# Packed weight tiles in layer 1, queries ahead of gates and values in the stick-breaking units, and each head's keys dealt out behind the queries of the head before

## The chip, the cores and the metric

The kernel runs on one core of one Trainium2 chip. The metric is the device time of one execution in microseconds (us), as the median of several. Everything is float32 in and out; a product of two float32 matrices is made of three matmuls of rounded parts (high x high, high x low, low x high), so each operand that enters TensorE is first split into a high and a low part.

## The reference, cut to what matters

Two layers over 16 learned meta tokens and 1024 tokens of width 1024. Layer 0 projects the input once and runs four heads of differential attention (A) and eight heads of stick-breaking attention (B) beside each other. Layer 1 is multi-head latent attention (C) of eight heads. Each has a gated output projection and a residual layer norm.

```python
def even_layer(x, ...):                       # layer 0
    qa, ka, va, ga, qs, ks, vs, gs = split_cols(x @ w_in, EVEN_SPLITS)
    ...
    # A: softmax of two maps, w = p[0] - lam * p[1]; rms_norm; * silu(ga)
    # B: z = q k / 8; skip = log_sigmoid(-z) over earlier keys
    log_pass = lax.cumsum(log_skip, axis=3, reverse=True) - log_skip
    a = jnp.where(earlier, jnp.exp(jax.nn.log_sigmoid(z) + log_pass), 0.0)
    ...
    return jnp.concatenate([ya, ys], axis=-1) @ w_out

def odd_layer(x, ...):                        # layer 1
    cq, ckv, k_pe, g = split_cols(x @ w_in, ODD_SPLITS)
    q = (rms_norm(cq, q_norm) @ w_uq).reshape(bsz, L, 8, 128 + 64)
    q = jnp.concatenate([q[..., :128], rope(q[..., 128:], pos)], axis=-1)
    kv = (rms_norm(ckv, kv_norm) @ w_ukv).reshape(bsz, L, 8, 128 + 128)
    ...
    return o @ w_out                          # after softmax, @ v, * silu(g)
```

## The kernel before

All tokens (1040 columns) stay in SBUF with the feature on the partitions. A projection (`project`, line 1941) is the product of one weight tile of 128 output features, with 8, 4 or 2 tiles of 128 input rows (`KT_OF`), and a chunk of 352, 344 or 344 columns (`CHUNKS`); each input tile costs three matmuls, so a chunk is 24, 12 or 6 matmuls. Projections go to two PSUM banks in turn, in their order in `PROJ` (`TURN_BANK`), and one may start once the step before the last has been evacuated (`bank_free`). ACT writes the high part (`proj_hi`) and DVE the low part (`proj_evac`).

Weight tiles (`WEIGHTS`, in order of use) are loaded by SP's queue into `wraw`, split by POOL (`split_weights`, lines 1032 and 1033) into `wsp`, and both have two slots. A split waits until the tile two places before in that order has been used up.

Layer 0 has eight units: 0 to 3 are the A heads, 4 to 7 are pairs of B heads. A unit has keys `k0`, values `v0`, queries `q0` and a gate `g0` of three chunks each, and the A units have a sum of squares `rms0` for a norm of their output. Of the queries there is one buffer, `qst`: a chunk is evacuated to half of its partitions, and POOL copies it to the others (`copy_queries`, line 1134) before scores (line 2009) may read it. For a B unit POOL also makes differences of neighbouring values (`step_values`) before the values are transposed (line 1980). Blocks of 128 queries are taken in pairs: scores of a block, sigmoid on ACT, a scan along the keys on DVE (line 1723), transposes of the weights on TensorE (line 2029), evacuation of these into `ring`, high part by ACT (line 1424) and low part by DVE (line 1738), and the product with the values (line 2059). The scores of blocks 5 to 7 need the third chunk of queries.

Layer 1 has, for each head u, keys `kn`, values `vn` and plain queries `qn`, and for each pair of heads rotated queries `qr`. A rotated chunk is copied by ACT into `rtmp` (line 1342), rotated there and spread by DVE (lines 1556 to 1609), and copied by POOL; there is one `rtmp`. `qh` is the buffer of the plain queries, written by ACT (line 1346) and DVE (line 1614), and is also single. The softmax weights are divided by their sum on POOL (line 1222).

`before_attention` and `in_attention` write down the order of the projections. `weave` then deals them out between the steps of the attention: it is a planner that plays all five engines with a cost for each step, and the order that comes out, for every engine, is fixed in the program. Projections are its fillers: TensorE takes one matmul of them where no score, transpose or product is ready. For the last two units it also deals out the first output blocks of the layer (`FILLS`: the meta block, called 8, and block 0, 48 matmuls of 512 columns each, line 2085), whose weights are eight tiles loaded and split in the meantime (`out_weight`, lines 1367, 1076 and 1777).

## Time and profile before

| | |
|---|---|
| median of 3 runs | 1376.29 us (1375.99 to 1381.58) |
| the profiled execution | 1376.59 us, its span 1374.8 us |
| layer 0: start, projections and attention | 0 to 660 us |
| layer 0 output blocks, layer 1 input projections, norms | 660 to 940 us |
| layer 1 attention | 940 to 1284 us, with some output work from 1270 us on |
| layer 1 output blocks | to the end |

Starts of rows are counted from the start of the span. A row that merges several instructions of one line gives their number behind x; the idle time in brackets is that of the engine just ahead of the row's first instruction, with what released it. PE is TensorE and PEld its weight loads, DVE is VectorE, ACT is ScalarE and POOL is GpSimd.

### The profile page before, as it was taken

The page shows a single profiled execution, that of the slowest core. Times are in us where ns is not written, and L with a number is a line of the kernel's source. Part 1 is how long each engine was busy: PE and PEld are TensorE (multiplying, and loading weights), DVE is VectorE, ACT ScalarE, POOL GpSimd, SP SyncE. Part 2 cuts the span into 40 slices and gives each one's busy share as a digit, 9 for nine tenths or more (in the row PEclk, how much of TensorE's full clock was granted, in tenths as well). Part 3 has the DMA queues.
Part 4 walks back from the last instruction along what each step waited for, and adds up shares of the span by engine and source line. Part 5 has one row for each costly group of instructions (what it writes and reads, how often), then busy time and mean ns, then how long its engine had stood idle before and what let it go on. Part 6 is the DMA issues. An engine that isn't in the chain of part 4 may idle for free.

```text
span 1374.8 us, 22469 instructions
## 1 busy us (share of the span) xinstructions
PE 1320.7 (96%) x8400; PEld 1243.6 (90%) x8400; DVE 874.2 (64%) x1973; ACT 546.1 (40%) x1290; POOL 487.3 (35%) x465
## 2 busy tenths in 40 slices
PE   8999999999899999997999999998999999999997
PEld 7999999999799999996888999998998999989886
DVE  5675869595587847668466323554767676676455
ACT  3443545463545535355111011533444555546200
POOL 3323232223234232347333323563433233334541
PEclk9999999999999999998999999999999999999999
DMA  6000111001011011113133211222111111205242
GB/s 221 32 32 31 47 32 40 23 31 47 32 39 40 20 43 51 60 40 123 58 123 132 93 46 41 83 81 73 36 47 39 51 41 58 66 22 177 78 163 76
DMA packets 47355, 88.26 MB, mean 64 GB/s; under 512 B 4480, under 2 KB 30080, under 8 KB 47120
## 3 DMA queue, kind: packets, MB, share of 16 engines
q1 hardware_dynamic: 44800, 78.45, 17.2%
q10 hardware_dynamic: 2448, 8.39, 1.6%
q8 instruction: 67, 1.10, 0.3%
q14 instruction: 40, 0.33, 0.1%
HBM read 66.84 MB, written 19.98 MB: 63 GB/s over the span
## 4 chain that ended last, share of the span: by engine, by line
PE 51%; DVE 5%; ACT 2%; issue 2%; POOL 1%; DMA 0%; SPq 0%; DVEq 0%; ACTq 0%; POOLq 0%
PE bank L1941 20%; PE bank L2085 14%; PE bank L2009 7%; PE bank L2059 5%; PE bank L2029 4%; ACT rtmp L1342 1%; PE bank L2107 1%; PE bank L1980 1%; DVE qpe L1605 0%; DVE rtmp L1558 0%; DVE qpe L1609 0%; DVE ring L1738 0%; DVE rtmp L1557 0%; DVE pb L1723 0%; DMA woraw<-in_wo 0%
## 5 line engine op out<-in xcount | busy, mean ns | idle before, releaser
L1941 PE MATMUL bank<-big,wsp 128*128 128x344 f32 (+2 forms) x3024 | 560.4, 328 | 15.2 <-DVE qh L1614 7.2
L1941 PEld LDWEIGHTS bank<-big,wsp 128*128 128x128 f32 x3024 | 481.7, 189 | 22.0 <-DVE qh L1614 10.5
L1032 POOL TENSOR_SCALAR wsp<-wraw 128x1024 fp32r<-128x1024 f32 (+3 forms) x92 | 84.9, 923 | 538.7 <-PE bank L1941 422.3
L1738 DVE TENSOR_TENSOR ring<-bank,ring 128x256 fp32r<-128x256 f32 (+3 forms) x292 | 156.9, 553 | 85.1 <-ACT ring L1424 82.5
L1424 ACT ACTIVATE ring<-bank 128x256 fp32r<-128x256 f32 (+3 forms) x292 | 138.6, 495 | 147.1 <-PE bank L2029 106.7
L2085 PE MATMUL bank<-big,wsp 128*128 128x512 f32 x816 | 195.9, 399 | 0.0
L1033 POOL TENSOR_TENSOR wsp<-wraw,wsp 128x1024 fp32r<-128x1024 f32 (+3 forms) x92 | 184.6, 2007 | 7.7
L2059 PE MATMUL bank<-ring,vtok 128*128 128x256 f32 (+2 forms) x1276 | 183.1, 280 | 4.2 <-DVE ring L1738 2.6
L2085 PEld LDWEIGHTS bank<-big,wsp 128*128 128x128 f32 x816 | 153.5, 190 | 35.1 <-DVE big L1777 0.2
L2059 PEld LDWEIGHTS bank<-ring,vtok 128*128 128x128 f32 (+1 forms) x1276 | 171.8, 191 | 10.0 <-issue 4.0
L1941 PE MATMUL bank<-h1t,wsp 128*128 128x344 f32 (+2 forms) x1080 | 173.9, 322 | 1.4 <-DVE lraw L1595 1.4
L1941 PEld LDWEIGHTS bank<-h1t,wsp 128*128 128x128 f32 x1080 | 170.2, 188 | 3.6 <-DVE lraw L1595 1.7
L2029 PE MATMUL bank<-eye,pb 128*128 128x128 f32 (+1 forms) x892 | 134.5, 274 | 11.3 <-DVE ring L1738 6.3
L2029 PEld LDWEIGHTS bank<-eye,pb 128*128 128x128 f32 (+1 forms) x892 | 103.1, 140 | 19.2 <-DVE ring L1738 8.3
L2009 PE MATMUL bank<-kst,qst 128*128 128x264 f32 (+9 forms) x480 | 104.3, 328 | 9.2 <-POOL qst L1134 8.2
L1723 DVE TENSOR_TENSOR_SCAN pb<-tb,distt 128x144 f32<-128x144 f32 (+4 forms) x72 | 100.6, 1409 | 5.6 <-PE bank L2029 3.7
L1222 POOL TENSOR_SCALAR pb<-pb,stat 128x144 f32<-128x144 f32 (+5 forms) x96 | 57.5, 609 | 109.7 <-DVE stat L1729 68.0
L2009 PEld LDWEIGHTS bank<-kst,qst 128*128 128x128 f32 x480 | 76.1, 189 | 21.2 <-POOL qst L1134 12.4
L1414 ACT ACTIVATE pb<-bank,stat 128x144 f32<-128x144 f32 (+6 forms) x112 | 59.7, 540 | 75.8 <-DVE stat L1694 57.8
L2009 PE MATMUL bank<-kh,qh 128*128 128x144 f32 (+6 forms) x336 | 73.4, 327 | 1.2 <-ACT pb L1414 0.8
L1805 DVE SCALAR_TENSOR_TENSOR res<-xres,bank 128x512 f32<-128x512 f32 (+1 forms) x34 | 21.9, 683 | 78.3 <-PE bank L2085 46.6
L1442 ACT ACTIVATE small<-small,eps 128x1 f32<-128x1 f32 (+1 forms) x17 | 5.0, 295 | 167.0 <-DVE small L1824 167.0
(133 smaller groups left out, 1432.5 us busy)
## 6 DMA issues: line engine op xcount, KB each, us to landing
wraw<-in_w SPq DMA_DIRECT2D x47, 512.0 KB, 3.5
wraw<-y_scratch SPq DMA_DIRECT2D x17, 448.0 KB, 3.6
woraw<-in_wo SPq DMA_DIRECT2D x12, 512.0 KB, 5.5
y_scratch<-ot SPq DMA_DIRECT2D x40, 128.0 KB, 1.7
xres<-in_x SPq DMA_DIRECT2D x8, 512.0 KB, 4.7
h_scratch<-res ACTq DMA_DIRECT2D x8, 512.0 KB, 2.6
gate_scratch<-gtmp SPq DMA_DIRECT2D x8, 512.0 KB, 2.9
gate<-gate_scratch SPq DMA_DIRECT2D x8, 512.0 KB, 3.6
```

Of the source, the lines that this page charges most:

```text
L1032: pool.wait_ge(S["pool_step"], tick(nc.gpsimd.tensor_scalar(hi, raw, 1.0, 1.0, ALU.mult, ALU.mult)))
L1033: return nc.gpsimd.tensor_tensor(lo, raw, lo_hi(hi), ALU.subtract)
L1222: nc.gpsimd.tensor_scalar(p_, p_, stat[:, t % 4, 13:14], 1.0, ALU.mult, ALU.mult)\
L1414: A(weights_of(1, slice(0, 128), g, slot, c0, c0 + w), bank[S_BANK[b]][:, 0:w], ACT.Exp, bias=st_(6, 7), scale=SCALE192, accum_out=st_(8 + ...
L1424: A(R[0:rows, r % NRING, 0, 0:w], bank[T_BANK[t]][0:rows, 0:w], ACT.Copy).then_inc(S["tr_hi"], 1)
L1723: V.tensor_tensor_scan(P[:, 0:n][:, ::-1], skip[:, ::-1], distt[0:rows, k0:k0 + n][:, ::-1], 1.0, ALU.mult, ALU.max).then_inc(S["p_ready_d ...
L1738: V.tensor_tensor(R[0:rows, r % NRING, 1, 0:w], bank[T_BANK[t]][0:rows, 0:w], lo_hi(R[0:rows, r % NRING, 0, 0:w]), ALU.subtract).then_inc( ...
L1941: ins = mm(dst, wsp[:, SLOT[kind, u], a, k, :], rhs[:, b, k0 + k, c0:c0 + w], start=(k == 0 and a == 0 and b == 0), stop=last)
L2009: ins = mm(dst, l, r, start=(k == 0), stop=(k == len(prods) - 1))
L2029: ins = nc.tensor.transpose(bank[T_BANK[t]][0:wide, at:at + rows], weights_of(layer, slice(0, rows), g, slot, k0, k0 + wide), eye[0:rows, ...
L2059: ins = mm(PO[:, o0:o0 + wide], l, B["ring"][0:rows, r % NRING, part, at:at + wide], start=(k == 0 and tile == turns[0][0] and part == 0 a ...
L2085: ins = mm(out_bank(n, half)[:, :], wsp[:, SLOT["y", n], a, k, :], wok[:, c, k, 512 * half:512 * half + 512], start=(k == tiles[0] and a = ...
```

## The change

Three things are changed, and no product is added or left out.

1. Layer 1's weight tiles are packed: keys and values of a head are one tile (`kv`, 4 input tiles), rotated and plain queries are one tile for an even head (`qq`, 8 input tiles), and an odd head's plain queries are a tile of 4. `TILE_STEPS` lists the projections that use a tile, and a slot is free after the last of them. Of 28 loads and splits in the attention of layer 1, 16 are left, of the same size together.
2. In layer 0, unit 4's queries stand around the gate of unit 3 (`q[:1] + g[:1] + q[1:] + g[1:]`), and in the B units each unit's next queries stand ahead of and between its values (`q[:1] + v[:1] + q[1:] + v[1:]`), where they stood behind all of them.
3. In layer 1, one chunk of the next head's keys stands behind each chunk of a head's queries, then come the values of the next head. In head 0 its own values take the place of the keys.

The host packs the weights into three arrays for this: `wukv[u]` (keys and values), `wuq_0` (even heads) and `wuq_1` (odd heads).

```diff
@@ -123,6 +123,19 @@
          "kn": KVL_T, "vn": KVL_T, "qn": QL_T, "qr": QL_T}
 
 
+def tile_of(kind, u):
+
+    return ("kv", u) if kind in ("kn", "vn") else ("qq", u) if kind in ("qn", "qr") else (kind, u)
+
+
+def tile_kt(kind, u):
+    return 2 * KVL_T if kind == "kv" else QL_T * (2 - u % 2) if kind == "qq" else KT_OF.get(kind, KD)
+
+
+def kt_before(kind, u):
+    return KVL_T if kind == "vn" else QL_T * (1 - u % 2) if kind == "qn" else 0
+
+
 def proj(kind, u):
     return [("P", kind, u, c) for c in range(len(CHUNKS))]
 
...
@@ -223,21 +236,35 @@
             k, v, q = (proj(kind, u + 1) if u + 1 < UNITS else [] for kind in ("k0", "v0", "q0"))
             norm = proj("rms0", u - 1) if 1 <= u <= A_UNITS else []
             g = proj("g0", u)
-            out += k + v[:1] + norm[:2] + v[1:2] + norm[2:] + v[2:] + proj("g0", u) + q if u < A_UNITS else k[:1] + norm + g[:1] + k[1:] + g[1:] + v + q
+            if u == A_UNITS - 1:
+                g = q[:1] + g[:1] + q[1:] + g[1:]
+                q = []
+            out += k + v[:1] + norm[:2] + v[1:2] + norm[2:] + v[2:] + g + q if u < A_UNITS else k[:1] + norm + g[:1] + k[1:] + g[1:] + q[:1] + v[:1] + q[1:] + v[1:]
         return out
-    out = queries(0, slice(0, None)) + proj("vn", 0)
-    for u in range(1, HEADS):
-        out += proj("kn", u) + proj("vn", u) + queries(u, slice(0, None))
+    out = []
+    for u in range(HEADS):
+        q, more = queries(u, slice(0, None)), proj("vn", 0) if u == 0 else []
+        more += proj("kn", u + 1) + proj("vn", u + 1) if u + 1 < HEADS else []
+        n = len(q) // len(CHUNKS)
+        for c in range(len(CHUNKS)):
+            out += q[n * c:n * c + n] + more[c:c + 1]
+        out += more[len(CHUNKS) * 1:]
     return out
 
 
 BEFORE, WITHIN = [before_attention(n) for n in range(2)], [in_attention(n) for n in range(2)]
 PROJ = [s for s in BEFORE[0] + WITHIN[0] + BEFORE[1] + WITHIN[1] if s[0] == "P"]
-TILES = [[s[1:3] for s in BEFORE[n] + WITHIN[n] if s[0] == "P" and s[1] != "rms0" and s[3] == 0] for n in range(2)]
+TILE_STEPS = {}
+for _s in PROJ:
+    if _s[1] != "rms0":
+        TILE_STEPS.setdefault(tile_of(*_s[1:3]), []).append(_s)
+TILES = [list(dict.fromkeys(tile_of(*s[1:3]) for s in BEFORE[n] + WITHIN[n] if s[0] == "P" and s[1] != "rms0"))
+         for n in range(2)]
 O_STEPS = [("O", 0, b) for b in [META_Q] + list(range(NB))] + [("O", 1, b) for b in range(NB)]
 O_AT = {s: n for n, s in enumerate(O_STEPS)}
 WEIGHTS = TILES[0] + [("y", n) for n in range(NB + 1)] + TILES[1] + [("y", n) for n in range(NB + 1, 2 * NB + 1)]
 WEIGHT_AT = {s: n for n, s in enumerate(WEIGHTS)}
+WEIGHT_AT |= {s[1:3]: WEIGHT_AT[tile] for tile, steps in TILE_STEPS.items() for s in steps}
 STATIONARY = WEIGHTS
 WO_ORDER = [list(range(KD)), [6, 7, 4, 5, 0, 1, 2, 3]]
 OUT_TILES = [[k for k in order if k < KD - 1] + [KD - 1] for order in WO_ORDER]
...
@@ -450,14 +477,14 @@
 
         kind, u = WEIGHTS[n]
         slot_of = WEIGHTS[n - 2]
-        end = ("P", *slot_of, 2) if slot_of[0] != "y" else O_STEPS[slot_of[1]]
+        end = TILE_STEPS[slot_of][-1] if slot_of[0] != "y" else O_STEPS[slot_of[1]]
         done = [("pe", end)] if end in within or end in FILLS[layer] else []
         stored = []
         if kind == "y":
             stored = [("sp", ("Y", unit_groups(layer, UNITS - 2)[-1]))]
         if n >= first_w + 2:
             L.put("sp", "L", ("LW", n), 65, ([("pool", ("V" if slot_of[0] == "y" else "W", n - 2))] if n - 2 >= first_split else []) + stored, 6500 if kind == "y" and layer else 4500)
-        kt = KT_OF.get(kind, KD)
+        kt = tile_kt(kind, u)
         L.put("pool", "W", ("W", n), 430 * kt, ([("sp", ("LW", n))] if n >= first_w + 2 else []) + done, 70)
         if kind == "y":
             last = ("Y", group_of(layer, O_STEPS[u][2]))
...
@@ -610,7 +637,7 @@
          for n in range(2) for k in range(KD)}
 PTURN = {s: n for n, s in enumerate(PROJ)}
 N_CONSTS = 6
-SLOT = {s: n % 2 for n, s in enumerate(STATIONARY)}
+SLOT = {s: n % 2 for s, n in WEIGHT_AT.items()}
 TURN_BEFORE, TURN_BANK = {}, {}
 _bank_turns = {}
 for _s in PROJ:
...
@@ -877,12 +904,9 @@
                 return w1[QL_T + KVL_T]
             if kind == "g1":
                 return w1[QL_T + KVL_T + 1 + u]
-            if kind == "qn":
-                return wuq_n[u]
-            if kind == "qr":
-                return wuq_r[u // 2]
-            return wukv[u, 0 if kind == "kn" else 1]
-
+            if kind == "qq":
+                return (wuq_1 if u % 2 else wuq_0)[u // 2]
+            return wukv[u]
 
         LAST0 = last_turn("g0", UNITS - 1)
         LAST1 = last_turn("qn", HEADS - 1)
...
@@ -911,7 +935,7 @@
                         dst = wraw[:, n % 2, 0:(KD - 1) * 128].rearrange("p (k c) -> p k c", k=KD - 1)
                         src = yd[layer, 0:KD - 1, :, c0:c0 + 128].rearrange("u p c -> p u c")
                     else:
-                        dst, src = wraw[:, n % 2, 0:KT_OF[kind] * 128], w_src(kind, u)
+                        dst, src = wraw[:, n % 2, 0:tile_kt(kind, u) * 128], w_src(kind, u)
                     sp.dma_start(dst, src).then_inc(slot("w_raw", n), 16)
                     issued[0] += 1
 
...
@@ -1038,14 +1062,14 @@
                     n = split_[0]
                     kind, u = WEIGHTS[n]
                     arrived(pool, "w_raw", n)
-                    kt, i = KT_OF.get(kind, KD - 1), STATIONARY.index((kind, u))
+                    kt, i = KD - 1 if kind == "y" else tile_kt(kind, u), STATIONARY.index((kind, u))
                     if i >= 2:
 
                         before = STATIONARY[i - 2]
                         if before[0] == "y":
                             pool.wait_ge(S["y_done"], before[1] + 1)
                         else:
-                            pool.wait_ge(S["proj_done"], last_turn(*before) + 1)
+                            pool.wait_ge(S["proj_done"], PTURN[TILE_STEPS[before][-1]] + 1)
                     ins = split(wsp[:, i % 2, 0, 0:kt, :], wsp[:, i % 2, 1, 0:kt, :],
                                 wraw[:, n % 2, 0:kt * 128].rearrange("p (k c) -> p k c", k=kt))
                     split_[0] += 1
...
@@ -1938,7 +1962,7 @@
                         pe.wait_ge(S["x_split"], X_FIRST[k, c0] + 1)
                     for a, b in ((0, 0), (0, 1), (1, 0)):
                         last = k == kt - 1 and a == 1
-                        ins = mm(dst, wsp[:, SLOT[kind, u], a, k, :], rhs[:, b, k0 + k, c0:c0 + w],
+                        ins = mm(dst, wsp[:, SLOT[kind, u], a, kt_before(kind, u) + k, :], rhs[:, b, k0 + k, c0:c0 + w],
                                  start=(k == 0 and a == 0 and b == 0), stop=last)
                         if last:
                             ins.then_inc(S["proj_done"], 1)
```

The planner makes a new order of all engines from this, beginning with the first queries of unit 4. From the product `X 86 0`, the first of the last head but for its early steps, TensorE's order is as before. Three places follow, all on TensorE, first as before and then as changed (line numbers of the changed kernel are 24 higher here).

The scores of unit 4 of layer 0: `big,wsp` is a projection, `sq,ones` a sum of squares, `kst,qst 128x392` the first scores that read the third chunk of queries. Before:

```order
L1941 MATMUL bank0<-big,wsp 128x352 x4
L2029 MATMUL bank6<-eye,pb 128x128 x2
L1941 MATMUL bank0<-big,wsp 128x352
L2029 MATMUL bank5<-eye,pb 128x128 x3
L1941 MATMUL bank0<-big,wsp 128x352 x19
L1954 MATMUL bank1<-sq,ones 128x352
L2009 MATMUL bank4<-kst,qst 128x392 x2
L2009 MATMUL bank2<-kst,qst 128x392 x2
L2009 MATMUL bank3<-kst,qst 128x328 x2
```

Changed:

```order
L2033 MATMUL bank3<-kst,qst 128x328 x2
L1965 MATMUL bank0<-big,wsp 128x344 x5
L2053 MATMUL bank6<-eye,pb 128x128 x2
L1965 MATMUL bank0<-big,wsp 128x344 x2
L2053 MATMUL bank5<-eye,pb 128x128 x3
L1965 MATMUL bank0<-big,wsp 128x344 x12
L1965 MATMUL bank1<-big,wsp 128x344
L2033 MATMUL bank4<-kst,qst 128x392 x2
L2033 MATMUL bank2<-kst,qst 128x392 x2
L2033 MATMUL bank3<-kst,qst 128x328 x2
```

Before, a chunk of keys of the next unit (128x352) and a sum of squares stand ahead of these scores; the third chunk of queries ends just ahead of the keys. Now a chunk of unit 3's gate (24 matmuls of bank 0, the last 19 of them here) and the first matmul of another stand there, and the queries ended ahead of that chunk.

The end of layer 0's attention, unit 7: `128x512` is the output block 8, `eye,pb` transposes of weights, `ring,vtok` products. Before:

```order
L2059 MATMUL bank7<-ring,vtok 128x256 x7
L2059 MATMUL bank7<-ring,vtok 128x128
L2059 MATMUL bank7<-ring,vtok 128x256
L2059 MATMUL bank7<-ring,vtok 128x128
L2029 MATMUL bank5<-eye,pb 128x128 x4
L2029 MATMUL bank6<-eye,pb 128x128 x3
L2029 MATMUL bank5<-eye,pb 128x128 x2
L2059 MATMUL bank7<-ring,vtok 128x256 x10
L2085 MATMUL bank0<-big,wsp 128x512 x3
L2085 MATMUL bank1<-big,wsp 128x512 x3
```

Changed:

```order
L2053 MATMUL bank6<-eye,pb 128x128 x2
L2109 MATMUL bank0<-big,wsp 128x512
L2053 MATMUL bank5<-eye,pb 128x128 x4
L2033 MATMUL bank4<-kst,qst 128x344 x2
L2033 MATMUL bank2<-kst,qst 128x344 x2
L2109 MATMUL bank0<-big,wsp 128x512 x2
L2109 MATMUL bank1<-big,wsp 128x512 x3
L2109 MATMUL bank0<-big,wsp 128x512
L2033 MATMUL bank3<-kst,qst 128x456 x2
L2033 MATMUL bank4<-kst,qst 128x456 x2
```

Before, the first output matmuls stand behind the last scores, among the transposes of the last pairs but one; now they begin ahead of the scores of 344 and 456 columns, and go on between all that follows.

The start of layer 1's attention, head 0: rotated (336 or 344 columns, 12 matmuls), plain (12) and, changed, values (6). Before:

```order
L1941 MATMUL bank0<-big,wsp 128x336 x12
L1941 MATMUL bank1<-big,wsp 128x336 x12
L1941 MATMUL bank0<-big,wsp 128x344 x12
L1941 MATMUL bank1<-big,wsp 128x344 x4
L2009 MATMUL bank2<-kh,qh 128x144 x3
L2009 MATMUL bank2<-kpe,qpe 128x144
L2009 MATMUL bank2<-kpe2,qpe 128x144
L2009 MATMUL bank3<-kh,qh 128x272 x3
L2009 MATMUL bank3<-kpe,qpe 128x272
L2009 MATMUL bank3<-kpe2,qpe 128x272
L1941 MATMUL bank1<-big,wsp 128x344 x8
L1941 MATMUL bank0<-big,wsp 128x344 x12
```

Changed:

```order
L1965 MATMUL bank0<-big,wsp 128x336 x12
L1965 MATMUL bank1<-big,wsp 128x336 x12
L1965 MATMUL bank0<-big,wsp 128x352 x6
L1965 MATMUL bank1<-big,wsp 128x344 x4
L2033 MATMUL bank2<-kh,qh 128x144 x3
L2033 MATMUL bank2<-kpe,qpe 128x144
L2033 MATMUL bank2<-kpe2,qpe 128x144
L2033 MATMUL bank3<-kh,qh 128x272 x3
L2033 MATMUL bank3<-kpe,qpe 128x272
L2033 MATMUL bank3<-kpe2,qpe 128x272
L1965 MATMUL bank1<-big,wsp 128x344 x8
L1965 MATMUL bank0<-big,wsp 128x344 x12
```

The rotated second chunk took bank 0, in which the rotated first chunk had been. It now takes bank 1, in which the plain first chunk was, and six matmuls of values (128x352) stand between.

## Rows read from the trace of the kernel before

**Rows 1.** The page: busy time, share of the span, instructions.

```profile
PE 1320.7 (96%) x8400; PEld 1243.6 (90%) x8400; DVE 874.2 (64%) x1973; ACT 546.1 (40%) x1290; POOL 487.3 (35%) x465
```

**Rows 2.** TensorE's waits, 300 to 660 us: total us, times, longest.

```profile
PE bank L2009 <- POOL qst L1134: 7.5, 6, 2.7
PE bank L2029 <- DVE ring L1738: 6.3, 5, 3.1
PE bank L1954 <- ACT sq L1354: 1.2, 1, 1.2
```

**Rows 3.** TensorE's waits, 938 to 1232 us.

```profile
PE bank L1941 <- DVE qh L1614: 7.2, 8, 1.7
...
PE bank L1941 <- DVE rtmp L1556: 1.3, 2, 0.6
PE bank L1941 <- POOL wsp L1033: 1.2, 1, 1.2
PE bank L2009 <- ACT pb L1414: 0.8, 1, 0.8
PE bank L1941 <- DVE kh L1612: 0.2, 1, 0.2
```

**Rows 4.** Timeline of TensorE: start, us, operation, count, idle before; first and last of four.

```profile
360.10 1.27 PE L2009 MATMUL bank<-kst,qst 128*128 128x392 f32 x6 [2.66 <-POOL qst L1134]
...
608.31 1.29 PE L2009 MATMUL bank<-kst,qst 128*128 128x392 f32 x6 [1.21 <-POOL qst L1134]
```

**Rows 5.** Windows: length, busy PE, PEld, DVE, ACT, POOL, clock, DMA, GB/s.

```profile
626.20:640.00 13.80, 10.14 (x57) 8.22 (x57) 10.67 (x16) 12.67 (x21) 13.44 (x8) 0.88 0.54 186
640.00:650.00 10.00, 6.37 (x38) 5.82 (x37) 9.94 (x10) 3.59 (x8) 10.00 (x3) 0.78 0.34 101
650.00:660.50 10.50, 10.50 (x64) 9.25 (x64) 6.75 (x10) 3.00 (x6) 5.12 (x3) 0.89 0.19 61
```

**Rows 6.** Timeline of TensorE, runs of one kind.

```profile
319.95 1.52 PE L2059 MATMUL bank<-ring,vtok 128*128 128x256 f32 x12
321.31 0.83 PE L2029 MATMUL bank<-eye,pb 128*128 128x128 f32 x6
...
576.67 13.38 PE L1941 MATMUL bank<-big,wsp 128*128 128x344 f32 x83
...
660.55 14.83 PE L2085 MATMUL bank<-big,wsp 128*128 128x512 f32 x63
```

**Rows 7.** Timeline of POOL in unit 4, and stepped values in unit 5.

```profile
353.77 3.22 POOL L1033 TENSOR_TENSOR wsp<-wraw,wsp 128x1024 fp32r<-128x1024 f32 x1
357.13 2.92 POOL L1134 TENSOR_SCALAR qst<-qst 64x688 fp32r<-64x688 f32 x2
...
415.32 1.92 POOL L1162 TENSOR_TENSOR sq<-vt 128x1039 f32<-128x1039 f32 x1
```

**Rows 8.** DVE's groups of 626.2 to 660.5 us, then timelines of DVE and POOL.

```profile
L1738 DVE TENSOR_TENSOR ring<-bank,ring 128x512 fp32r<-128x512 f32 (+2 forms) x18 | 10.1, 590 | 4.7 <-ACT ring L1424 4.7
...
634.45 2.31 DVE L1723 TENSOR_TENSOR_SCAN pb<-tb,distt 128x1040 f32<-128x1040 f32 x1
...
641.98 3.64 DVE L1723 TENSOR_TENSOR_SCAN pb<-tb,distt 128x1040 f32<-128x1040 f32 x1
...
636.98 2.36 POOL L1076 TENSOR_TENSOR big<-pre_values,big 128x1024 fp32r<-128x1024 f32 x1
639.30 11.78 POOL L1076 TENSOR_TENSOR big<-woraw,big 128x1024 fp32r<-128x1024 f32 x3
```

**Rows 9.** Timelines of ACT and DVE, head 0's second rotated and plain chunks.

```profile
951.75 1.83 ACT L1342 ACTIVATE rtmp<-bank 32x344 f32<-32x344 f32 x4 [2.57 <-DVE qpe L1609]
...
953.61 0.52 DVE L1556 TENSOR_TENSOR rtmp<-bank,ropet 128x344 f32<-128x344 f32 x1 [1.42 <-ACT rtmp L1342]
...
956.91 0.52 DVE L1614 TENSOR_TENSOR qh<-bank,qh 128x344 fp32r<-128x344 f32 x1
```

**Rows 10.** Timeline of POOL: the split of a tile of 4 input tiles.

```profile
974.98 1.28 POOL L1033 TENSOR_TENSOR wsp<-wraw,wsp 128x512 fp32r<-128x512 f32 x1
```

14 lines of the change are left out of this document (8 added, 6 removed).

## The prediction

> **What bounds the kernel now.** I read the page first. TensorE is busy for 96% of the span, its weight loads for 90%, no other engine for over 64% [rows 1]. So time is won or lost only where TensorE stands still, or where its matmuls run at less than the full granted clock. Next come the waits of TensorE: in the four attention units of the second group (B) and at the end of layer 0 it waits 7.5 us for POOL's copies of queries and 6.3 us for DVE's half of the turned weights (`ring`); in layer 1 it waits 7.2 us for `qh`, 1.3 us for `rtmp` and 1.2 us for a split weight tile [rows 2, 3]. Third, the timeline of TensorE, to place them: four long waits for copied queries stand once in each B unit, before the 128x392 scores [rows 4]. Fourth, the last 34 us of layer 0's attention by windows: the loads fill 8.2 of 13.8 us, 5.8 of 10.0 and 9.2 of 10.5, and the granted clock is 0.88, 0.78 and 0.89, so parts of it run at 1.2 GHz, right after TensorE had stood still [rows 5]. Elsewhere a run of bare projections goes at 13.38 / 83 = 0.161 us a matmul and output products at 14.83 / 63 = 0.235 us [rows 6].
>
> **Layer 0, queries sooner.** What makes the copy of a unit's third chunk of queries late is POOL's order: the long half of a split, 3.22 us, is ahead of the copy, which takes 2.92 [rows 7], and 24 key projections hide only a part. Now the copy stands ahead of that split; in unit 4 as many gate projections (first order excerpt, 3.9 us) and four more score tiles stand between the queries and the scores that read them, in units 5 to 7 two chunks of values or more. The four waits, 2.66 us the first, 1.21 the last [rows 4], with the two between them 7.05 of the 7.5 us in [rows 2], go: **-7.05 us** (bounds -7.5 and -4, if half comes back as waits for DVE's scans).
>
> What is late next. (a) The three sums of squares of unit 3 now stand in a row, so the third and the gate behind it wait for ACT's logarithms with no scores between. One such wait is 1.2 us now [rows 2]; I take it twice: **+1.2**. (b) In units 5 and 6 the gate tile takes the slot that the last value chunk leaves, and only 24 key matmuls (3.9 us) hide a split of about 1.1 us and up to 3.22, with POOL's stepped values, 1.92 us and two small steps, behind it, on which the value transposes wait [rows 7]: 0.7 for each split, 0.7 for the transposes: **+2.1** (0 to +5).
>
> **The end of layer 0.** Gates of the last unit are finished sooner, and output blocks 8 (meta) and 0 fill the tail: 85 of their 96 matmuls stand before the last product, against 26 now. I count from the last gate projection (626.2 us) until block 0 is done. Before: 34.3 us, then 70 products x 0.235 = 16.4, in all 50.7. After, 7.8 us of attention move behind that point: 7 score tiles x 0.42 (1.28 us for three, [rows 4]), 22 products x 0.113 (12 in 1.36 us between starts, 319.95 to 321.31, [rows 6]), 24 transposes of half the columns x 0.1. TensorE's work behind it is 85 x 0.235 = 20.0, products 96 x 0.113 = 10.9, transposes 78 x 0.105 = 8.2, scores 2.9: 42 us. DVE's is eight scans, by columns of 2.31 us for 1040 in all 15; 25 `ring` subtractions of 10.1 / 18, 14; outputs, one gate chunk and two output weights, by its 27.4 busy us now less four scans and 18 subtractions and for three outputs more, 10: 39 us [rows 5, 8]. Both are near full, and POOL contends: the same scan takes 2.31 us, and 3.64 while POOL copies, and POOL's copy 2.36, but 11.78 / 3 = 3.93 beside the scans [rows 8]. I take 49 us (bounds 45 and 55), then 11 x 0.235 = 2.6. So 51.6 - 7.8 = 43.8 against 50.7: **-7** (bounds -11 and -1). The half-speed stretches are in this.
>
> Layer 0 in all: -7.05 + 1.2 + 2.1 - 7.0 = **-10.7 us** (-17 to -2).
>
> **Layer 1, packing.** POOL splits the same columns in 16 tiles, not 28; splits and loads are hidden except at two places. Head 0: the wait of 1.2 us for the second queries' tile goes [rows 3], the larger first tile ends some 0.4 later than its first product. The keys of head 1 now need a tile whose slot is free only after the last values of head 0, which stand right before them: a split of 0.6 + 1.28 us [rows 10] and two hand-overs, 2.1 us. In later heads at least 12 query products and some attention lie between, 4 us against 2.1: nothing.
>
> **Layer 1, a third of keys behind each third of queries.** This is the term that decides. Projections use two banks in turn, so a step waits for the evacuation of the step before the last. In the heads with rotated queries (0, 2, 4, 6) a third was rotated (12), plain (12), and is now rotated, plain, keys (6; in head 0 values). A rotated chunk costs ACT 1.83 us, then DVE from 953.61 to 957.43, the plain chunk's `qh` last [rows 9]: 0.15 + 1.83 + 0.1 + 3.8 = 5.9 us from the rotated projection's end until the plain one's bank is free, 6.2 to 7 with other DVE work. Before, that bank was asked for after plain + rotated, 2 x 1.95 = 3.9 us of matmuls; now after plain + keys, 2.9 us. The reader sees the banks in the third excerpt: the rotated chunk now takes bank 1, which the plain one just left.
> - Head 0: first third 0.5 + 2.4 us (nothing else is in between), second 0.6 + 2.4, third 2.1 (the split above, same place), 0.4 at the start: 8.4. Waited now: 1.2 + 1.7 + 0.8 + 0.2 = 3.9 [rows 3]. **+4.5**.
> - Heads 2, 4, 6 have one order. Into the three gaps fall 2.1, 1.3 and 2.3 us of attention. Waits: 5.9 - 5.1 = 0.8; 6.1 - 4.3 = 1.8; 7.3 - 5.2 = 2.1: 4.7 a head, 14.1. Waited now: 7.2 - 1.7 of `qh`, 1.3 of `rtmp`, 6.8 [rows 3]. **+7.3**.
> - Odd heads: 0.95 us of keys against 1.2 us of evacuation, mostly with attention between: 0.
> While TensorE waits the others run ahead, and small waits behind it go: -1.6. Layer 1: **+10 us** (+2, if the fillers cover all but the split; +14).
>
> **Sum.** -10.7 + 10 = -0.7. The profiled execution took 1376.59 us with a span of 1374.8; 1376.6 - 0.7 = 1375.9, and the median of the runs is 0.3 lower: **1375.5 us**.
>
> A rule speaks to the tail. The row shows a scan of 3.64 us beside POOL's copies, against 2.31 [rows 8]. The Trainium skill, "SBUF — State Buffer", section on SBUF's two separate sides, has DVE operations with two SBUF inputs and GpSimd operations exclude each other for a whole instruction. The lengthening agrees; taken strictly it gives rival 3.
>
> **Rivals.**
> 1. *Layer 1 is covered.* The attention between the thirds fills the 5.9 us, since the heads' scores and transposes become ready while TensorE waits, and the waits only change place. Then layer 1 costs +1 and layer 0 stands: 1376.3 - 10.7 + 1 = 1366.6, 1360 to 1369. For it: in head 2 only 2.1 us are waited now, though the chain is the same. Against: in head 0 nothing is there to fill, and instructions run in a fixed order.
> 2. *Slower: the two-bank turn at its full price.* If DVE's other work falls into the chain each time, a third lasts rotated 1.95 + 6.2 = 8.2 us; with 4.9 us of projections in it, 3.3 us are waited, 12 x 3.3 = 40, against 10.7 now: +29, less 10.7: 1376 + 18 = 1394. It decides from the point where 2.4 us a third are lost instead of 1.9 (12 x 2.4 - 10.7 + 2 = +20, 1385). TensorE standing still so often could also lower its granted clock, as in the tail, at 0.78 [rows 5].
> 3. *The tail does not shorten.* Eight scans, each 1.3 us longer behind POOL's copies: DVE 39 + 10.4, with hand-overs of 4 us 54; the tail gives -2, and 1376.3 - 7.05 + 3.3 - 2 + 10 = 1380.5.
> 4. *It does not do what it says.* Sooner queries are of no use where the scans set the pace; half of the 7.05 us comes back elsewhere, with the rest as forecast: 1379.
>
> **How the numbers follow.** Forecast 0.48, its own range 1368 to 1382 (the half gaps of both terms); rival 1 0.22; rival 2 0.17; rivals 3 and 4 together 0.13. The bound of 0.5%, about what a measurement of this kernel tells from no change, lies at 6.9 us: 1369.4 and 1383.2. Faster: rival 1 and 0.04 of the forecast, 0.26. Slower: rival 2 and 0.02 of the forecast, 0.19. Same: 0.55. The range 1362 to 1387 holds the forecast, rivals 3 and 4, nearly all of rival 1 and the near end of rival 2.
>
> **What will show it.** The four waits before the 128x392 scores are gone, right; one of over 1 us left, wrong. Windows from the last gate to the last product of layer 0: 49 us with clock near 1.00. In layer 1 the waits of TensorE's projections for `qh` rise from 7.2 to about 18 us in total, in clumps of 1 to 2.5 us before a rotated chunk, and one of 2 us for `wsp` before the keys of head 1. If `qh` stays under 10, rival 1 holds; above 28, rival 2. I am wrong altogether if layer 0 up to the first output block after the attention is not some 11 us earlier.

## The result and the profile after

The changed kernel takes **1413.84 us** (median of 4 runs, 1410.95 to 1416.93) against 1376.62 us before: 2.7% slower, ratio 1.027 with a 95% interval of 1.025 to 1.029. The forecast was 1375.5 us with a range of 1362 to 1387, so the time lies 27 us outside of it, further than the rival that ended on the slow side (1394).

Four marks that stand in both orders divide the 37.2 us between the two spans (1374.8 and 1412.0). Starts are those of the profiled executions: the first scores of unit 0, the first output transposes of layer 0 (`eye,res`), the first and the last `kh,qh` scores of layer 1.

| | before | changed | difference |
|---|---|---|---|
| start to the first scores | 41.12 | 38.61 | -2.5 |
| layer 0 from there to the output transposes | 646.9 | 657.8 | **+10.9** (forecast -10.7) |
| to the first scores of layer 1 | 264.9 | 264.0 | -0.9 |
| layer 1 attention | 314.8 | 344.5 | **+29.7** (forecast +10) |
| to the end | 107.0 | 107.1 | +0.1 |

The -2.5 is no part of the change, whose order is the same there: of the traces of this study eleven have their first scores at 38.3 to 39.6 us, and three at 41.1 to 41.4, among them that of before.

The page's line of busy times has to be read with care here. It answers to [rows 1]:

```profile
PE 1335.1 (95%) x8400; PEld 1257.0 (89%) x8400; DVE 883.1 (63%) x1973; ACT 547.9 (39%) x1290; POOL 482.1 (34%) x441
```

The same 8400 matmuls have become 14.4 us longer (1320.7 before). The other 22.8 us are idle time. So the loss has two parts, standing still and running slowly. The waits of TensorE (line, engine and tile waited for; us in total, times, longest), first from 300 to 690 us, then from 940 to 1290; they answer to [rows 2, 3]:

```profile
PE bank L2033 <- POOL qst L1158: 9.7, 6, 2.8
PE bank L2053 <- DVE ring L1762: 7.8, 3, 4.8
PE bank L2033 <- ACT tb L1417: 3.4, 3, 1.3
```

```profile
PE bank L1965 <- DVE qh L1638: 27.4, 12, 3.6
PE bank L1965 <- DVE rtmp L1580: 1.2, 2, 0.7
```

With the smaller groups, TensorE's idle time is 26.1 us in the first stretch (18.3 before) and 29.9 in the second (14.8 before). The waits for copied queries did not go, they rose; those for `qh` rose from 7.2 us to 27.4.

The second part shows in windows of 2.5 us over the whole span. I add up (1 - granted clock) x length of the windows; at 1.2 GHz, half of 2.4, that sum is the full-speed work that was not done. From 300 to 700 us it is 5.2 before and 8.5 now; in the attention of layer 1 it is 0.0 before and 15.4 now. Two places, around a wait before the first scores of unit 5 (407.16) and around one in head 2 (1081.55); columns as in [rows 5]:

```profile
402.50:407.50 5.00, 3.31 (x25) 2.75 (x24) 4.96 (x7) 1.58 (x3) 3.43 (x2) 1.00 0.00 0
407.50:412.50 5.00, 5.00 (x27) 4.94 (x27) 1.45 (x3) 0.35 (x2) 0.00 (x0) 0.66 0.00 0
...
1077.50:1082.50 5.00, 1.43 (x7) 1.18 (x6) 4.53 (x8) 0.46 (x1) 2.60 (x4) 0.81 0.30 105
1082.50:1087.50 5.00, 5.00 (x16) 4.85 (x16) 1.30 (x4) 0.27 (x1) 0.00 (x0) 0.50 0.07 26
```

In the second and in the last row TensorE is "busy" for all 5.00 us, but does 27 and 16 matmuls in them: the clock is what is low. The two parts nearly add up. In layer 0, 7.8 idle + 3.3 clock = 11.1 against +10.9. In layer 1, between the marks of the table, TensorE is idle for 27.6 us where it was 11.2: 16.4 + 15.4 = 31.8 against +29.7. That is 2.1 too much, 0.7 of it because the clock was also low while TensorE stood still, where it costs nothing.

**Layer 0, place by place.** The starts of the units in TensorE's timeline:

```profile
317.11 0.89 PE L2033 MATMUL bank<-kst,qst 128*128 128x16 f32 x6 [0.89 <-POOL qst L1158]
...
351.61 1.29 PE L2033 MATMUL bank<-kst,qst 128*128 128x392 f32 x6 [2.83 <-POOL qst L1158]
...
407.16 0.89 PE L2033 MATMUL bank<-kst,qst 128*128 128x16 f32 x6 [1.69 <-POOL qst L1158]
...
492.94 1.05 PE L2033 MATMUL bank<-kst,qst 128*128 128x16 f32 x6 [2.04 <-POOL qst L1158]
...
577.66 0.89 PE L2033 MATMUL bank<-kst,qst 128*128 128x16 f32 x6 [2.04 <-POOL qst L1158]
```

Against [rows 4]: the long waits before the 128x392 scores of units 5 to 7 are gone, as forecast. The one of unit 4 stayed, 2.83 us for 2.66, and the prediction had called one of over 1 us a sign of being wrong. And units 5 to 7 now wait at their first scores (128x16), for the first chunk of queries. POOL's copy of that chunk in unit 5, now and then in the kernel before:

```profile
403.59 3.52 POOL L1158 TENSOR_SCALAR qst<-qst 64x704 fp32r<-64x704 f32 x2 [3.42 <-DVE qst L1600]
```

```profile
419.49 1.64 POOL L1134 TENSOR_SCALAR qst<-qst 64x704 fp32r<-64x704 f32 x2 [0.85 <-DVE qst L1576]
```

A chunk is copied by two instructions. They take 3.52 us now, beside a scan of DVE (403.87, 2.66 us), and the scores start 0.05 us after they end. Before, the same two took 1.64 us with no scan beside them. Units 6 and 7 are alike: 3.57 for 1.64. From the end of the queries' projection to the scores it is 5.9, 5.8 and 5.8 us, where it was 3.9, 4.2 and 4.2. The copies are 1.9 us longer, and the waits are 1.7, 2.0 and 2.0. In the order, these scores stand 17, 15 and 15 matmuls of projections behind the first chunk of queries in units 5, 6 and 7, where it was 8, 23 and 23; unit 5 waits though it has more of them than before.

**Layer 1, head 2.** TensorE's timeline, the three waits of one head with rotated queries (heads 4 and 6 have the same to 0.02 us):

```profile
1049.81 0.74 PE L1965 MATMUL bank<-big,wsp 128*128 128x344 f32 x3 [0.96 <-DVE qh L1638]
1063.42 1.41 PE L1965 MATMUL bank<-big,wsp 128*128 128x344 f32 x4 [2.10 <-DVE qh L1638]
1081.55 1.51 PE L1965 MATMUL bank<-big,wsp 128*128 128x352 f32 x4 [3.57 <-DVE qh L1638]
```

and what DVE and POOL do ahead of the third:

```profile
1076.20 0.52 DVE L1580 TENSOR_TENSOR rtmp<-bank,ropet 128x344 f32<-128x344 f32 x1 [1.30 <-ACT rtmp L1366]
1076.63 0.51 DVE L1581 TENSOR_TENSOR rtmp<-rtmp,ropet 128x344 f32<-128x344 f32 x1
1077.18 0.95 DVE L1582 TENSOR_TENSOR rtmp<-rtmp 128x344 f32<-128x344 f32 x1
1078.16 1.63 DVE L1629 CAST qpe<-rtmp 64x344 fp32r<-64x344 f32 x2
1079.82 1.03 DVE L1633 TENSOR_TENSOR qpe<-rtmp,qpe 64x344 fp32r<-64x344 f32 x2
1080.88 0.52 DVE L1638 TENSOR_TENSOR qh<-bank,qh 128x344 fp32r<-128x344 f32 x1
```

```profile
1077.14 0.62 POOL L1056 TENSOR_SCALAR wsp<-wraw 128x512 fp32r<-128x512 f32 x1 [1.84 <-PE bank L1965]
1077.84 1.40 POOL L1057 TENSOR_TENSOR wsp<-wraw,wsp 128x512 fp32r<-128x512 f32 x1
```

Rotation and `qh` take DVE 5.20 us from 1076.20, where [rows 9] had 3.8. The two steps that are longer, 0.95 (0.52 for the like step at 967.32) and 1.63 (0.68 at 967.87), lie beside POOL's split; at 967 POOL was idle.

### The profile page after: what moved, and what is told of

Same layout as the page of the kernel before. It is cut to its first block, busy times and chain, and to the rows that moved or that the text cites. A ratio compares the mean times of both kernels' runs of the same rounds, so it can differ in the third digit from the quotient of the medians.

```text
span 1412.0 us, 22424 instructions
## 1 busy us (share of the span) xinstructions
PE 1335.1 (95%) x8400; PEld 1257.0 (89%) x8400; DVE 883.1 (63%) x1973; ACT 547.9 (39%) x1290; POOL 482.1 (34%) x441
## 4 chain that ended last, share of the span: by engine, by line
PE 77%; DVE 11%; ACT 4%; issue 3%; POOL 3%; DMA 1%; SPq 0%; DVEq 0%; ACTq 0%; POOLq 0%
PE bank L1965 37%; PE bank L2109 13%; PE bank L2033 11%; PE bank L2083 8%; PE bank L2053 6%; POOL qst L1158 2%; DVE pb L1747 2%; ACT rtmp L1366 1%; PE bank L2004 1%; DVE qpe L1633 1%; DVE ring L1762 1%; DVE qpe L1629 1%; DMA wraw<-in_w 1%; DVE qst L1600 1%; POOL wsp L1057 1%
## 5 line engine op out<-in xcount | busy, mean ns | idle before, releaser
L1965 PE MATMUL bank<-big,wsp 128*128 128x344 f32 (+2 forms) x3024 | 570.2, 331 | 33.2 <-DVE qh L1638 27.4
L1965 PEld LDWEIGHTS bank<-big,wsp 128*128 128x128 f32 x3024 | 487.0, 191 | 42.1 <-issue 17.1
L1056 POOL TENSOR_SCALAR wsp<-wraw 128x1024 fp32r<-128x1024 f32 (+2 forms) x80 | 80.9, 1012 | 466.8 <-PE bank L1965 355.4
L2109 PE MATMUL bank<-big,wsp 128*128 128x512 f32 x816 | 199.2, 399 | 0.0
L1057 POOL TENSOR_TENSOR wsp<-wraw,wsp 128x1024 fp32r<-128x1024 f32 (+2 forms) x80 | 180.1, 2252 | 6.7
L2033 PE MATMUL bank<-kst,qst 128*128 128x264 f32 (+9 forms) x480 | 110.6, 334 | 14.6 <-POOL qst L1158 10.3
L2033 PEld LDWEIGHTS bank<-kst,qst 128*128 128x128 f32 x480 | 79.0, 193 | 26.9 <-POOL qst L1158 14.4
L1699 DVE TENSOR_REDUCE stat<-bank 128x1 f32<-128x144 f32 (+6 forms) x112 | 56.4, 508 | 36.5 <-PE bank L2033 35.2
L2033 PE MATMUL bank<-kh,qh 128*128 128x144 f32 (+6 forms) x336 | 78.7, 345 | 0.1
L1158 POOL TENSOR_SCALAR qst<-qst 64x688 fp32r<-64x688 f32 (+1 forms) x48 | 45.6, 950 | 84.8 <-DVE qst L1600 81.7
```

Source lines behind the costliest of these rows:

```text
L1056: pool.wait_ge(S["pool_step"], tick(nc.gpsimd.tensor_scalar(hi, raw, 1.0, 1.0, ALU.mult, ALU.mult)))
L1057: return nc.gpsimd.tensor_tensor(lo, raw, lo_hi(hi), ALU.subtract)
L1158: ins = nc.gpsimd.tensor_scalar(to, lo_hi(from_), 1.0, 1.0, ALU.mult, ALU.mult)
L1965: ins = mm(dst, wsp[:, SLOT[kind, u], a, kt_before(kind, u) + k, :], rhs[:, b, k0 + k, c0:c0 + w], start=(k == 0 and a == 0 and b == 0), s ...
L2033: ins = mm(dst, l, r, start=(k == 0), stop=(k == len(prods) - 1))
L2109: ins = mm(out_bank(n, half)[:, :], wsp[:, SLOT["y", n], a, k, :], wok[:, c, k, 512 * half:512 * half + 512], start=(k == tiles[0] and a = ...
```

## The experiments

All kernels were compared with the kernel before on the same chip, in three groups; its median was 1376.77 us beside the first four, 1378.28 beside the second four and 1376.06 beside the last. Ratios are to these. A difference between two runs is that of their medians as they stand; across two groups, up to 2.2 us of it can be the difference of the groups.

### The parts, one at a time

**e1, layer 0's part alone.** The diff is part 2 of the change:

```diff
+            if u == A_UNITS - 1:
+                g = q[:1] + g[:1] + q[1:] + g[1:]
+                q = []
...
-  ... k[:1] + norm + g[:1] + k[1:] + g[1:] + v + q
+  ... k[:1] + norm + g[:1] + k[1:] + g[1:] + q[:1] + v[:1] + q[1:] + v[1:]
```

> The kernel before with the layer 0 part of the change alone (queries ahead of gates and values from unit 4 on); layer 1 is as before. Theory (the two parts add up, and the trace of the changed kernel shows what each costs): from the first scores of unit 0 to the output transposes of layer 0 the changed kernel took 657.8 us (38.61 to 696.43), the kernel before 646.9 (41.12 to 688.06). So 10.9 us slower, 1387.5 us (1384 to 1391): TensorE waits for copied queries about 2 us before the first scores (128x16) of units 5, 6 and 7 and runs at half its clock after each. Rival (the prediction's: queries sooner and a filled tail gain, and what was lost in layer 0 comes from something else in the program): 1366 to 1372 us.

Measured: 1387.98 us, ratio 1.0077 (1.0056 to 1.0097), +11.2 us. The waits from 300 to 690 us are those of the changed kernel, to the number:

```profile
PE bank L2012 <- POOL qst L1137: 9.7, 6, 2.8
PE bank L2032 <- DVE ring L1741: 7.8, 3, 4.8
PE bank L2012 <- ACT tb L1396: 3.4, 3, 1.3
```

**e2, packing alone.** `tile_of`, `tile_kt`, `kt_before` and `TILE_STEPS` of the change, with both layers' projections in the order of before.

> The kernel before with packed weight tiles in layer 1 alone; the order of the projections is as before in both layers. Theory: the packing costs nothing, the loss of layer 1 is the dealing out of the keys: 1376 us (1374 to 1379). Rival (the packed tiles' larger splits and later slots are what TensorE waits for, and the waits for qh are a consequence): over 1385 us.

Measured: 1380.24 us, ratio 1.0026 (1.0017 to 1.0036), +3.5 us: 1.2 us above the theory's range, far below the rival's. Packing is not free, since the planner makes another order from it too: layer 1's attention takes 322.6 us in the trace, 7.8 more than before, with one wait for `qh` of 3.25 us and 3.4 us lost to half clock right behind it.

**e3, layer 1's part alone** (parts 1 and 3 of the change).

> The changed kernel with layer 0 as it was before: packed tiles and a third of the next head's keys behind each third of a head's queries. Theory (the parts add up): from the first to the last head's first-form score rows of layer 1 the changed kernel took 344.5 us (960.42 to 1304.94), the kernel before 314.8 (952.98 to 1267.80), so 29.7 us slower, 1406 us (1401 to 1409), with about 27 us of waits for qh and a granted clock of about 0.66 in the stretches behind them. Rival (the late start of layer 1 in the changed kernel brought it into another phase): under 1395 us, near the 1386 of my forecast's +10.

Measured: 1408.27 us, ratio 1.0226 (1.0201 to 1.0251), +31.5 us. Waits for `qh` 27.3 us in 12, 17.1 us lost to half clock in layer 1. Two single parts give 11.2 + 31.5 = 42.7 us, 5.5 more than both together, about what the three intervals allow (some 3 us to either side each). TensorE's order in layer 0 is the same in e1 and in the changed kernel, and so are the waits above, but the trace of e1 loses 12.0 us to the clock there and that of the changed kernel 8.5. So the changed kernel is slow because each of its two reorderings is, and dealing out the keys costs 28 us beyond the packing.

### What it is in layer 1

**e4, the keys between the thirds multiplied twice.** This puts more work on TensorE at the very places where it waits:

```diff
+TWICE = {("vn", 0), ("kn", 3), ("kn", 5), ("kn", 7)}
...
+                for k in [*range(kt)] * (times - 1):
+                    for a, b in ((0, 0), (0, 1), (1, 0)):
+                        mm(dst, wsp[:, SLOT[kind, u], a, kt_before(kind, u) + k, :], rhs[:, b, k0 + k, c0:c0 + w],
+                           start=(k == 0 and a == 0 and b == 0), stop=(k == kt - 1 and a == 1))
```

> The kernel of e3_layer1_only in which the values of head 0 and the keys of heads 3, 5 and 7, those that stand between thirds of rotated and plain queries, are each multiplied twice (the same six matmuls twice into the same bank, the first result thrown away): 12 chunks x 6 = 72 matmuls more, 72 x 0.161 = 11.6 us of TensorE's work. Theory (what is lost is that the step between the plain third and the next rotated third has only 0.95 us of matmuls where it had 1.95, so TensorE waits for the bank of the plain third; with 1.95 us the wait is as before, and fewer long waits also leave the clock up): no slower than e3_layer1_only, rather 0 to 12 us faster, with waits for qh down from 27 to about 15 us. Rival (the heads' work on DVE sets the pace, TensorE's waits are only where it shows): 0 to 3 us slower with unchanged ends. Second rival (waits stand elsewhere in the queue and the work simply adds): 10 to 12 us slower.

Measured: 1395.67 us, ratio 1.0135 (1.0120 to 1.0150): with 72 matmuls more the kernel is **12.6 us faster** than e3. The waits of the projections in layer 1, and the only long one left in head 2:

```profile
PE bank L1971 <- DVE qh L1638: 12.1, 8, 2.6
PE bank L1963 <- DVE rtmp L1580: 2.2, 2, 1.5
```

```profile
1062.70 1.10 PE L1971 MATMUL bank<-big,wsp 128*128 128x344 f32 x6
1066.44 0.88 PE L1971 MATMUL bank<-big,wsp 128*128 128x352 f32 x4 [2.65 <-DVE qh L1638]
```

This shows two things. The lack is of matmuls between a plain third and the next rotated one: with 1.95 us there instead of 0.95 the waits for `qh` fall by 15.2 us (in head 2 from 0.97, 2.09 and 3.55 to none, 0.69 and 2.65), and all idle time of TensorE from 940 to 1290 us by 13.5 (32.2 to 18.7). And the clock is a cost of its own: had only the idle time changed, 13.5 - 11.6 = 1.9 us would be gained; the clock's loss in layer 1 fell from 17.1 to 5.1, and 1.9 + 12.0 = 13.9 is near the measured 12.6. The rival in which DVE sets the pace is out. The planner counted the doubled steps and made its order anew, so a part of this can come from another placing of the attention; no run holds the order fixed.

**e7, keys dealt out behind odd heads only.**

```diff
+        if u % 2 == 0:
+            out += q + more
+            continue
...
+            out += q[c:c + 1] + more[c:c + 1]
...
```

> Packed tiles in layer 1 with a third of the next head's keys behind each third of the queries of the odd heads (1, 3, 5) alone, where a third is plain queries only; in heads 0, 2, 4 and 6 the queries stand together as before; layer 0 as before. Theory (only where rotated queries stand is the dealing out dear, since the plain third's bank is asked for after 2.9 instead of 3.9 us of matmuls): as e2_pack_only, 1378 to 1383 us, waits for qh 7 to 11 us. Rival (any key chunk among queries costs): half of the 28 us by which e3_layer1_only is behind e2_pack_only, 1390 to 1398 us.

Measured: 1372.85 us, ratio 0.9966 (0.9952 to 0.9980), 5.4 us faster than before and 7.4 faster than e2, under the 1378 to 1383 of the theory. Waits for `qh` 5.5 us in 4. The same dealing out that costs 28 us in all heads costs nothing where a third is plain queries alone. That it should gain anything I had not expected. In the trace layer 1's attention takes 315.8 us, against 314.8 before and 322.6 in e2, so e7 only takes back what packing had cost there. The rest of the trace's gain over before lies in the start (2.5 us), which the change does not touch, and behind layer 1's attention (104.6 us to the end for 107.0).

**e8, e3 with the planner's price of a rotated chunk set to the trace's.**

```diff
-                "kn": (360, 440), "qn": (360, 440), "qr": (1450, 2700)}.get(kind, (0, 440))
+                "kn": (360, 440), "qn": (360, 440), "qr": (1850, 3400)}.get(kind, (0, 440))
```

> The kernel of e3_layer1_only (packed, all keys dealt out, layer 0 as before) in which the planner reckons a rotated chunk at 1850 ns on ACT and 3400 on DVE, as the trace of before has them, instead of 1450 and 2700. The order of the projections stays, only the attention between them can be placed otherwise. Theory (the lack is of matmuls between the thirds, and a planner that knows the chain can put attention there where it has some): waits for qh from 27.3 down to 20 to 24 us, 2 to 8 us faster than e3_layer1_only: 1400 to 1406 us. Rival (there is no attention ready to be put there): within 2 us of 1408. If it falls below 1390, the loss was the planner's misjudgement and not the order of the projections.

Measured: 1404.87 us, ratio 1.0184 (1.0154 to 1.0213), 3.4 us less than e3, waits for `qh` 25.5 us. The planner knew too little of the chain, but that is a small part; by the rival's reading there is hardly any attention to put between the thirds, which this fits and doesn't prove.

### What it is in layer 0

**e5, the planner's price of a copy of queries set near the trace's,** on top of e1:

```diff
-            L.put("pool", "Q", s, 1400 if kind == "q0" else 900, [("dve", s)], 70)
+            L.put("pool", "Q", s, 3000 if kind == "q0" else 900, [("dve", s)], 70)
```

> The kernel of e1_layer0_only (layer 0's new order of projections, layer 1 as before) with one number of the planner changed: it reckons POOL's copy of a chunk of queries at 3000 ns, near the 3.52 us that the trace of the changed kernel shows at 403.59, instead of 1400. In units 6 and 7 the first scores then stand 25 projections behind the first chunk of queries instead of 15, and in unit 4 the scores of the third chunk 34 behind it instead of 25. Theory (the four waits only moved from the third chunk to the first, because the first scores were put too close behind a copy that the planner thinks short; each wait of 2 us also brings about 2 us at half clock): the waits for copies before the 128x16 scores fall from 5.8 us in all to under 1.5, the stretches at half clock behind them go, and the kernel is 6 to 12 us faster than e1_layer0_only: 1376 to 1382 us. Rival (DVE's scans set the pace of a unit, and a wait taken away here comes back at the scores or the turned weights): 1385 to 1389 us.

Measured: **1367.06 us**, ratio 0.9907 (0.9883 to 0.9932): 20.9 us faster than e1, where 6 to 12 were expected, and faster than the kernel before. POOL and TensorE at the start of unit 5:

```profile
393.34 3.52 POOL L1137 TENSOR_SCALAR qst<-qst 64x704 fp32r<-64x704 f32 x2 [3.42 <-DVE qst L1579]
```

```profile
394.18 2.65 PE L1944 MATMUL bank<-big,wsp 128*128 128x352 f32 x15
396.91 0.89 PE L2012 MATMUL bank<-kst,qst 128*128 128x16 f32 x6
```

The copy takes the same 3.52 us and ends at 396.86; but 15 matmuls of projection stand right ahead of the scores, where the changed kernel has 5, and the scores start at 396.91 with no wait. All waits for copies in the stretch are 1.1 us, where they were 9.7, idle time falls from 27.3 to 16.5, and the clock's loss from 12.0 to 3.4: 10.8 + 8.6 = 19.4 of the 20.9 us. 1.9 us of it lie in units 0 to 2, where both have the old order of projections. So more than half of what layer 0 lost in e1 came of scores set too close behind a copy that the planner reckons at 1.4 us and that takes 1.6 to 4.5. The new order of projections has a cost of its own: of the 11.2 us of e1, 4.8 are left when both orders are planned with 3000 ns (e5 behind e6, which follows).

**e6, the same number in the kernel before,** nothing else.

> The kernel before with the same one number (3000 ns for 1400) and nothing else. Theory: the waits for copied queries of 7.5 us between 300 and 660 us fall under 3 us without any change of the order of the projections: 1370 to 1374 us. Rival (scans set the pace): 1375 to 1379 us.

Measured: **1362.24 us**, ratio 0.9875 (0.9851 to 0.9899), 16.0 us faster than before by one number, and 8 us beyond the theory's range. Of the traces' 13.5 us, 2.5 are the start again and 12.7 lie in layer 0 (634.3 us from the first scores to the output transposes, for 646.9); from 300 to 690 us idle time fell by 5.1 and the clock's loss by 1.8. 1.9 more lie in units 0 to 2. The rest of some 4 us is not idle time: the page has 1314.8 us of busy time for the same 8400 matmuls, 1320.7 before [rows 1], so they run denser in the new mixture of kinds. Why, no view told, and it stays open. So the waits for copies explain a part of the 16 us and not all of it: the number also gave another order.

### Together

**e9, e7 with the planner's copy at 3000 ns.**

> The kernel of e7_odd_heads (packed tiles, keys dealt out in odd heads alone, layer 0's order of projections as before) with the planner's copy of queries at 3000 ns as in e6_before_copy_cost: both edits were faster than before, each in another layer. Theory (they add): 16 + 5 us, 1355 to 1360 us. Rival (the two share a gain, such as a stretch at half clock that either removes): 1361 to 1364 us.

Measured: **1359.47 us**, ratio 0.9875 (0.9852 to 0.9898). That is in the theory's range, just, but only 16.6 us under before on its own chip, where 16 + 5 were to add up. The ratio is that of e6. In the traces e9 is 4.0 us under e6, 3.3 of them outside both stretches of attention, as in e7. The lowest time of the study, but by the medians not to be told from e6, and e6 needs no packing.

**e10, e9 with layer 0's new order.**

> The whole changed kernel, layer 0's new order of projections too, with two faults taken out: the planner's copy at 3000 ns, and no keys between the thirds of heads 0, 2, 4 and 6. Theory: the layer 0 part is worth nothing once the copy is priced rightly (e5 was 5 us behind e6), so 4 to 6 us slower than e9_odd_copy3000: 1360 to 1366 us. Rival (the new order and the odd heads help each other): equal to it or faster.

Measured: 1364.65 us, ratio 0.9909 (0.9884 to 0.9934), 5.2 us behind e9: with the copy priced rightly, layer 0's new order is still worth less than the old. In the traces layer 0 from the first scores on takes 637.4 us for 634.5 here, and 637.5 for 634.3 in e5 and e6.

**e11, e9 with the copy at 2200 ns.**

> As e9_odd_copy3000 with 2200 ns, half way between the old value and the new, in the planner. The traces of before and after show 1.6 to 3.5 us for a copy. Theory (what counts is that the scores stand behind the copy's real end, and 2200 leaves those copies uncovered that fall beside a scan): waits for copies of 1 to 3 us left, 0 to 5 us slower than e9_odd_copy3000. Rival (any value over 1400 rearranges the units as well, the gain is from that): the same within 1 us, or faster, with waits left.

Measured: 1368.17 us, ratio 0.9940 (0.9919 to 0.9962), 8.7 us behind e9, where 0 to 5 were expected. One wait for a copy of 1.7 us is left, as the theory has it, but the loss is larger: new waits of 3.9 us for POOL's copies of output weights have come. A number in a planner moves more than the step that it prices. At 1400, 2200 and 3000 ns the ratios are 0.9966 (e7), 0.9940 and 0.9875 (e9); no higher value was run.

**e12, e9 with the rotated chunk priced as in e8.**

> As e9_odd_copy3000 with the planner's price of a rotated chunk at 1850 ns on ACT and 3400 on DVE as in e8_qr_cost. Theory (a rightly priced chain lets attention stand where TensorE would wait): 1 to 4 us faster than e9_odd_copy3000, waits for qh under 5 us. Rival (nothing is ready to stand there, as e8 showed with 3.4 us of 28): within 1 us.

Measured: 1362.10 us, ratio 0.9901 (0.9871 to 0.9931), 2.6 us behind e9. The two intervals overlap, but each run of e12 took longer than each of e9 (1362.03 and more, 1360.14 and less). Waits for `qh` rose from 5.5 to 11.4 us. Both expectations missed; a truer price didn't bring a better order.

## Why the prediction was wrong

**Layer 0, queries sooner: -7.05, measured none of it.** The step that failed is "now the copy stands ahead of that split", with the conclusion that the four waits go. For units 5 to 7 it was right for the third chunk of queries and was not asked of the first: all three chunks came sooner relative to the values, but the planner put the first scores 15 to 17 projections behind the first chunk. I read only the 128x392 scores of the order. For unit 4 it was wrong even for the third chunk: two copies took 4.51 us, 2.92 before [rows 7], behind a DVE evacuation that came late, and 25 matmuls of projections stood between, 24 before. What the prediction took as given is the length of a copy and not only its place. In units 5 to 7 the first chunk's copy, now beside a scan, takes 3.5 us for 1.64, and that 1.9 us is the whole wait: with a copy of 1.64 the same order would have left 0.2 us or less, by subtraction from these rows. That the scan is what lengthens the copy rests on the two standing side by side in all three units; no run took the scan away. The prediction said of POOL's copies of output weights that they lengthen beside scans [rows 8], and did not ask it of the copies of queries.

**Late next: +3.3, measured +4.1.** Waits other than for `qst` and `ring` were 4.5 us from 300 to 690 us and are 8.6, under other names than forecast: one behind the sums of squares (1.52, for `kst`), three for ACT's sigmoids (`tb`, 3.4 in all), 0.7 each for values (`vtok`) and a split.

**The tail: -7, measured -2.** From the last gate projection (628.8 us) until block 0 is done (685.0) it is 56.2 us, forecast 51.6, before 50.7. Less the 7.8 us of attention that moved behind that point, by the prediction's own count, that is 48.4 for 50.7. The stretch ahead, from the first scores to that gate projection, was to lose these 7.8 us and 3.7 more; it is 5.1 us longer. Apart from the 7.8 it is 12.9 us longer than before, where it was to be 3.7 shorter. Three windows of that stretch, columns as in [rows 5]:

```profile
628.80:640.00 11.20, 4.83 (x31) 4.24 (x30) 9.60 (x10) 9.52 (x15) 10.83 (x8) 0.86 0.66 228
640.00:650.00 10.00, 9.97 (x47) 8.29 (x45) 8.18 (x9) 5.67 (x11) 9.92 (x6) 0.81 0.02 4
650.00:685.00 35.00, 33.47 (x212) 29.04 (x210) 27.71 (x37) 13.39 (x27) 15.08 (x9) 1.00 0.26 74
```

From 650 us on it went as forecast, TensorE full and clock 1.00. The loss is in the first 21 us: output matmuls were meant to fill them, but 31 matmuls stand in the first 11.2 us, and the first output matmul starts at 638.20. What the output reads was only just written: a copy of its weights by DVE until 635.72, a split by POOL until 637.17. DVE copied one in 3.41 us while POOL did the same with another, and the turned weights waited behind it for 4.8 us:

```profile
632.31 3.41 DVE L1801 TENSOR_TENSOR big<-pre_keys,big 128x1024 fp32r<-128x1024 f32 x1 [0.23 <-ACT big L1391]
635.65 1.51 DVE L1747 TENSOR_TENSOR_SCAN pb<-tb,distt 128x656 f32<-128x656 f32 x1
```

The estimate summed each engine's work over the whole tail and never asked when the fillers become ready. And "the half-speed stretches are in this" was too kind, the clock was 0.86 and 0.81 there.

**Layer 1: +10, measured +29.7.** The mechanism was named rightly, bank by bank. Its terms, by size: head 0, forecast 8.4 us of waits, measured 0.47 + 0.68 + 1.96 + 0.48 + 2.10 + 3.45 = 9.1. The wait of 2.1 us for the split before head 1's keys came as one for `qh` of 3.45 at the same place. Heads 2, 4, 6: forecast 0.8, 1.8 and 2.1 in each, measured 0.96, 2.10 and 3.57; the third was mis-sized, since DVE's part of the chain is 5.2 us beside POOL's split and not 3.8. That is 19.9 for 14.1. The waits of the projections are so 18.3 us more where 11.8 were forecast. The -1.6 for small waits behind them came too, and more: from 940 to 1300 us TensorE's waits at other steps are 1.5 us, 4.9 before. By its idle time alone layer 1 would be at +16.4 between its marks.

**What was left out is the clock: +15.4 in layer 1 and +3.3 in layer 0.** I had the rows for it, 0.88, 0.78 and 0.89 in the tail [rows 5], and put it as a half sentence into rival 2. Of the nine waits of 1.9 us or more in layer 1 eight have a stretch at half clock behind them. Rival 2 was the nearest: its mechanism is what happened, but its price put everything on the waits (3.3 us a third) and nothing on the clock. Measured are 27.4 us of `qh`, just under the 28 from which I had said it would hold.

**The chances.** That 0.17 stood for the slow side came from weighing the two parts against each other, -10.7 against +10, as though both were sure. The slow side had two ways to come about, the gain of layer 0 failing and the loss of layer 1 growing; the range should have held both at once, 1376 + 3 + 14 = 1393 at the least.

## What to carry to other kernels

If a work item is moved sooner, look in the order at every reader of it, the first one above all, and compare the work between with the measured length of the whole hand-over. Where an order comes from a planner with costs, compare these costs with the trace before anything is rearranged: one stale number (1.4 us for a copy of 1.6 to 4.5) was worth 16 us here, more than the 10.7 forecast for the rearrangement. A step that is moved can change its length: ask what the other engines do in its new place. Work of half the size between two long steps that share two banks was a loss here, without one instruction more, where the hand-over of a bank took longer than the matmuls between; in the odd heads, where it did not, it cost nothing. And waits of about 2 us and more on a full TensorE cost up to twice their length in layer 1 of the changed kernel (16.4 idle, 15.4 clock), though not each of them.
